# Transformer stack in float32, first block's mixer: another order of projection chunks and attention steps, turns one step later, grouped heads paired; extra constant matmuls at three places

## The reference, cut to what matters

```python
for l in range(DEPTH):                         # DEPTH = 2
    h = rms_norm(x, pre_mix_norm[l])
    proj = jnp.einsum('bsd,de->bse', h, w_in[l])       # 1024 -> 2464 columns
    (na_q, na_k, na_v, df_q, df_k, df_v, gq_q, gq_k, gq_v,
     ml_cq, ml_ckv, ml_kr) = jnp.split(proj, offsets, axis=-1)
    a_out = neighbourhood_attention(..., rel_bias[l])  # 4 heads of 64, with a bias
    b_out = diff_attention(dq[0], dq[1], dk[0], dk[1], ..., lam, slopes)
    b_out = rms_norm(b_out, diff_subln[l]) * (1.0 - lambda_init)
    c_out = gqa_attention(cq, ck, ...)                 # 4 query heads on 2 key heads
    d_out = mla_attention(q_nope, q_rope, k_nope, k_rope, mla_v)
    mix = jnp.concatenate([a_out, b_out, c_out, d_out], axis=-1)
    x = x + rms_norm(mix @ w_o[l], post_mix_norm[l])
    ...                                        # gated MLP, norm, residual
```

## Time and profile before

| | us |
|---|---|
| median of 3 runs | 1963.43 (1956.75 to 1965.12) |
| the profiled execution, its own time | 1959.28 |
| its span, first to last instruction | 1957.5 |
| PE busy in the span | 1867.2 (95%) |
| DVE busy | 1138.0 (58%) |
| ACT busy | 921.6 (47%) |
| mean granted TensorE clock | 0.981 |
| mixer of layer 0, from 84.67 to 132.91 | 48.24 |
| mixer of layer 1, from 430.22 to 481.12 | 50.90 |

### The profile page before, as it was taken

One profiled execution on the slowest core, in us unless ns is written; L12 is line 12 of the kernel. 1 busy time (PEld: TensorE's weight loads), 2 busy tenths in 40 slices (PEclk: granted clock), 3 DMA queues, 4 the chain that ended last, 5 costly groups with the idle time before them and its releaser, 6 DMA issues. The chain is left out here.

```text
span 1957.5 us, 29109 instructions
## 1 busy us (share of the span) xinstructions
PE 1867.2 (95%) x11568; PEld 1634.4 (83%) x11568; DVE 1138.0 (58%) x1647; ACT 921.6 (47%) x1267; POOL 175.0 (9%) x213
## 2 busy tenths in 40 slices
PE   7899999988999999899999999999889999989998
PEld 6668999766899978689998789998669998769997
DVE  6676555757655578554446465446765546765443
ACT  4564334456434446554435355345245435564342
POOL 1300000040000030001000001002501002000000
PEclk9999999999999999799999999999989999989999
DMA  7504555550355555126555425554725554524551
GB/s 249 181 22 147 175 183 185 181 172 12 129 193 193 191 187 180 49 87 215 176 204 177 172 86 175 201 182 169 219 90 172 173 202 147 203 91 173 181 204 66
DMA packets 185356, 313.08 MB, mean 160 GB/s; under 512 B 18877, under 2 KB 67571, under 8 KB 185267
## 3 DMA queue, kind: packets, MB, share of 16 engines
q1 hardware_dynamic: 182595, 304.24, 46.0%
q0 software_dynamic: 1376, 4.38, 0.9%
q10 hardware_dynamic: 1296, 3.24, 0.5%
HBM read 309.90 MB, written 1.94 MB: 159 GB/s over the span
## 5 line engine op out<-in xcount | busy, mean ns | idle before, releaser
L1459 DVE TENSOR_TENSOR w_lo<-raw,w_hi 128x2048 fp32r<-128x2048 f32 (+2 forms) x290 | 654.0, 2285 | 289.7 <-ACT w_hi L995 289.0
L995 ACT ACTIVATE w_hi<-raw 128x2048 fp32r<-128x2048 f32 (+2 forms) x290 | 533.5, 1877 | 107.5 <-PE tr L2010 59.8
L2008 PE MATMUL acc<-w_hi,hT_hi 128*128 128x512 f32 (+2 forms) x688 | 270.1, 393 | 13.3 <-DVE w_lo L1459 7.3
L2010 PE MATMUL acc<-w_hi,hT_lo 128*128 128x512 f32 (+2 forms) x688 | 266.4, 387 | 0.0
L2009 PE MATMUL acc<-w_lo,hT_hi 128*128 128x512 f32 (+2 forms) x688 | 266.3, 387 | 0.0
L2008 PE MATMUL acc<-w_hi,aux_hi 128*128 128x512 f32 x608 | 237.2, 390 | 0.0
L2009 PE MATMUL acc<-w_lo,aux_hi 128*128 128x512 f32 x608 | 237.2, 390 | 0.0
L2010 PE MATMUL acc<-w_hi,aux_lo 128*128 128x512 f32 x608 | 236.6, 389 | 0.0
L2008 PE MATMUL up<-hT_hi,w_hi 128*128 128x256 f32 x768 | 217.8, 284 | 0.6 <-DVE w_lo L1459 0.6
L2009 PE MATMUL tr<-hT_lo,w_hi 128*128 128x256 f32 x768 | 217.5, 283 | 0.0
L2008 PE MATMUL tr<-hT_hi,w_hi 128*128 128x256 f32 x768 | 217.5, 283 | 0.0
(11 more groups left out here) (361 smaller groups left out, 2761.1 us busy)
## 6 DMA issues: line engine op xcount, KB each, us to landing
raw<-in_mlp_w_up SPq DMA_DIRECT2D x64, 1024.0 KB, 6.6
raw<-in_mlp_w_down SPq DMA_DIRECT2D x64, 1024.0 KB, 5.4
raw<-in_ffn_w_gate_up SPq DMA_DIRECT2D x88, 512.0 KB, 4.8
raw<-in_ffn_w_down SPq DMA_DIRECT2D x22, 1024.0 KB, 5.1
raw<-in_w_in SPq DMA_DIRECT2D x16, 1024.0 KB, 8.2
raw<-in_sb_w_in SPq DMA_DIRECT2D x12, 1024.0 KB, 5.3
raw<-in_moba_w_in SPq DMA_DIRECT2D x12, 1024.0 KB, 5.3
raw<-in_nsa_w_in SPq DMA_DIRECT2D x10, 1024.0 KB, 6.3
```

The source lines that it names most:

```text
L995: nc.scalar.activation(w_hi[:, p0.slot, 0:p0.floats], raw[:, p0.slot, 0:p0.floats], ACT.Copy)\
L1459: nc.vector.tensor_tensor(w_lo[:, p0.slot, 0:m], raw[:, p0.slot, 0:m], f32(w_hi[:, p0.slot, 0:m]), ALU.subtract).then_inc(sem["lo_ready"], 1)
L2008: nc.tensor.matmul(dst, hi, whi, start=first, stop=False)
L2010: return nc.tensor.matmul(dst, lo, whi, start=False, stop=last)
```

## The change

1. The chunks of `w_in` are projected in the order (4, 3, 2, 1, 0). `jobs_early` now turns the differential q and k in place of the neighbourhood ones, which are the two late jobs now.
2. The scores of the first two steps are issued by PE inside the last chunk, behind `jobs_early` (`STEPS_EARLY = 2`); DVE (`steps_early`) and ACT take their maxima and exponentials there, ahead of emptying the last chunk.
3. The step order is DF and GQ, then NA, then ML. The turns are three steps behind the scores and the products four (`TURN_LAG = 3`). The two late jobs stand behind turn(1), ahead of out(0).
4. The differential norm is cut in three: ACT copies and squares (`od_taken`, now two increments), DVE reduces, takes the root and multiplies in three consecutive iterations; `diff_turn` stands in iteration 19 and writes the bank that the DF sums held.
5. The grouped heads are laid out so that the two heads of a step write different halves; POOL uses three additions in place of one for that.
6. ACT's exponential for `lam` moves from the mixer's head to behind chunk 3.
7. `keep_clock` is added in the last attention stage (10, ahead of the fifth turning job), in the stick-breaking stage (5, ahead of the first sums) and behind the convolution's variance (16).

```diff
-STEP_ORDER = (0, 1, 2, 3, 4, 5, 12, 6, 7, 13, 8, 9, 14, 10, 11, 15, 16, 17, 18, 19)
+STEP_ORDER = (4, 12, 5, 13, 6, 7, 14, 8, 9, 15, 10, 11, 0, 1, 2, 3, 16, 17, 18, 19)
+TURN_LAG = 3
...
+STEPS_EARLY = 2
...
-            g1 = add_gemm(plan, A["w_in"][l], D, A_IN, "proj", (4, 3, 0, 1, 2), {2: up_projections})
+            g1 = add_gemm(plan, A["w_in"][l], D, A_IN, "proj", (4, 3, 2, 1, 0), {2: up_projections})
...
-            g2.order = (0, 1, 4, 5, 2, 3, 6, 7)
+            g2.order = (4, 5, 2, 3, 0, 1, 6, 7)
...
+        def turn_index(j):
+            return JOBS_EARLY + j if j < STEPS_EARLY else JOBS_A + j
...
-                pair([head(half_rows(8 + t, HD * u, HD), half_rows(10, HD * u, HD), col("gq_v") + HD * u, HD * t, 4 + u)
-                      for u in range(2)])
+                pair([head(half_rows(8 + t, HD * u, HD), half_rows(10, HD * u, HD), col("gq_v") + HD * u,
+                           HD * (t if u == 0 else 1 - t), 4 + u) for u in range(2)])
```

ACT in the last chunk and in the mixer:

```diff
+                        for j in range(STEPS_EARLY):
+                            pair_exp(pair_steps()[j], j)
...
+                for i in range(STEPS_EARLY, len(steps) + TURN_LAG + 1):
                     if i < len(steps):
+                        pair_exp(steps[i], i)
+                    if 0 <= i - TURN_LAG < len(steps):
+                        j = i - TURN_LAG
...
+                    if i == STEPS_EARLY + TURN_LAG - 1:
+                        for j in range(JOBS_EARLY, JOBS_A):
+                            _, dst, scale = jobs_for("A")[j]
+                            evac_job(j + STEPS_EARLY, dst, scale, n["pt_ready"])
...
+                    if i == DF_LAST + 5:
+                        act.wait_ge(sem["o_done"], n["o_done"] + DF_LAST + 1)
+                        nc.scalar.activation(h[:, 0, 0:512], acc[:, 1, :], ACT.Copy).then_inc(sem["od_taken"], 1)
+                        nc.scalar.activation(h[:, 0, 512:1024], acc[:, 1, :], ACT.Square).then_inc(sem["od_taken"], 1)
+                    if i == DF_LAST + 8:
+                        act.wait_ge(sem["hT_tr"], n["hT_tr"] + 1)
+                        pair_out_hi((2, 3))
```

DVE (`steps_early` runs in the last chunk, before DVE empties its sums):

```diff
+            def steps_early(l):
...
+                for i in range(STEPS_EARLY):
+                    pair_max(steps[i], i)
+                    if i:
+                        pair_scaled(steps[i - 1], i - 1)
...
+                def diff_sums():
+
+                    dve.wait_ge(sem["od_taken"], n["od_taken"] + 2)
+                    sq = h[:, 0, 512:1024].rearrange("p (a c) -> p a c", c=HD)
+                    link(nc.vector.tensor_reduce(ss[:, 16:24], sq, AX_X, ALU.add))
...
+                    if i == DF_LAST + 5:
+                        diff_sums()
                     if i == DF_LAST + 6:
+                        diff_root()
+                    if i == DF_LAST + 7:
                         diff_gain()
...
+                    if i == DF_LAST + 8:
+                        pair_out_lo((2, 3), 4)
```

PE:

```diff
+                for i in range(STEPS_EARLY):
+                    pe.wait_ge(sem["pt_evac"], n["pt_evac"] + 2 * (i + 1))
+                    pair_scores(pair_steps()[i], i)
...
+                    if i == STEPS_EARLY + TURN_LAG - 1:
+                        late_jobs()
+                    if i == DF_LAST + 8:
+                        diff_turn()
+                    if i > TURN_LAG:
+                        j = i - TURN_LAG - 1
...
                         if j == ML_FIRST:
-                            pe.wait_ge(sem["od_taken"], n["od_taken"] + 1)
+                            pe.wait_ge(sem["hT_lo"], n["hT_lo"] + 4)
...
+                    if j == 4:
+                        pe.wait_ge(sem["evac_a"], n["evac_a"] - 1)
+                        pe.wait_ge(sem["evac_d"], n["evac_d"] - 1)
+                        keep_clock(acc[:, 0, 0:S], 10)
...
+                    if heads[0] == 0:
+                        keep_clock(acc[:, 0, 0:S], 5)
...
                 last.then_inc(sem["var_ready"], 1)
+                keep_clock(tr[:, 0, 0:S], 16)
```

More of the change, by code:

```diff
@@ L587, in pair_steps @@
                            A_IN + 128 * (2 * t + u) + 64, HD * u, 6 + t) for u in range(2)])
-            for i in range(GQ_STEPS.start, GQ_STEPS.stop):
-                steps[i]["apart"] = False
             return [steps[i] for i in STEP_ORDER]
@@ L1517, in gemm @@
                         turned_lo(ph.then, range(KT // 2))
+                    if ph.mix is not None and ph.mix.kind == "mixA" and i == 4:
+                        steps_early(ph.mix.l)
                     dve.wait_ge(sem["piece_used"], pieces[-1][0] + 1)
@@ new lines, in steps_early, with pair_max @@
+                for i in range(STEPS_EARLY):
+                    pair_max(steps[i], i)
+                    if i:
+                        pair_scaled(steps[i - 1], i - 1)
+            def pair_max(step, i):
+                slot = i % 4
+                dve.wait_ge(sem["s_ready"], n["s_ready"] + i + 1)
+                if step["bias"] is None:
+                    nc.vector.tensor_reduce(nmx[:, 2 * slot:2 * slot + 2], pair_banks(i), AX_X, ALU.min)\
+                        .then_inc(sem["s_max"], 1)
+                else:
+                    for u in range(2):
+                        ins = nc.vector.tensor_tensor_reduce(
+                            prob[:, slot, u, :], pair_bank(i, u), step["bias"][u], -step["scale"], -LOWEST, ALU.add,
+                            ALU.min, nmx[:, 2 * slot + u:2 * slot + u + 1])
+                    ins.then_inc(sem["s_max"], 1)
@@ new lines, in pair_scaled @@
+            def pair_scaled(step, i):
+                slot = i % 4
+                c = slice(2 * slot, 2 * slot + 2)
+                dve.wait_ge(sem["p_exp"], n["p_exp"] + 2 * (i + 1))
+                link(nc.vector.reciprocal(rec[:, c], den[:, c]))
+                p0, p1 = prob[:, slot, 0, :], prob[:, slot, 1, :]
+                r0, r1 = (rec[:, 2 * slot + u:2 * slot + u + 1] for u in range(2))
+                if step["diff"] is not None:
+                    mark(nc.vector.tensor_scalar(r1, r1, lam[:, 4:5], None, ALU.mult))
+                    link(nc.vector.tensor_scalar(p0, p0, r0, None, ALU.mult))
+                    nc.vector.scalar_tensor_tensor(out=p1, in0=p1, scalar=r1, in1=p0, op0=ALU.mult, op1=ALU.add)\
+                        .then_inc(sem["p_norm"], 2)
+                else:
+                    nc.vector.tensor_scalar(p0, p0, r0, None, ALU.mult).then_inc(sem["p_norm"], 1)
+                    nc.vector.tensor_scalar(p1, p1, r1, None, ALU.mult).then_inc(sem["p_norm"], 1)
@@ L2105, in jobs_early, with pair_scores @@
                     job(j, jobs_for("A")[j][0], n["pt_evac"])
+                for i in range(STEPS_EARLY):
+                    pe.wait_ge(sem["pt_evac"], n["pt_evac"] + 2 * (i + 1))
+                    pair_scores(pair_steps()[i], i)
+            def pair_scores(step, i):
+                for u, head in enumerate(step["heads"]):
+                    last = nc.tensor.matmul(pair_bank(i, u), head["q"][:, P * step["qt"]:P * step["qt"] + P], head["k"],
+                                            start=True, stop=True)
+                last.then_inc(sem["s_ready"], 1)
             def lag_turn():
@@ L2293, in mix_A @@
                 steps = pair_steps()
-                for i in range(len(steps) + 3):
+                for i in range(STEPS_EARLY, len(steps) + TURN_LAG + 1):
                     if i < len(steps):
                         step = steps[i]
-                        if i >= 2 and steps[i - 2]["bias"] is not None:
+                        if steps[i - 2]["bias"] is not None:
                             pe.wait_ge(sem["s_max"], n["s_max"] + i - 1)
-                        elif i >= 2:
+                        else:
                             pe.wait_ge(sem["p_exp"], n["p_exp"] + 2 * (i - 1))
-                        for u, head in enumerate(step["heads"]):
-                            last = nc.tensor.matmul(pair_bank(i, u), head["q"][:, P * step["qt"]:P * step["qt"] + P], head["k"],
-                                                    start=True, stop=True)
-                        last.then_inc(sem["s_ready"], 1)
-                    if i == 1:
-                        diff_jobs()
-                    if 2 <= i < len(steps) + 2:
-                        j = i - 2
-                        pe.wait_ge(sem["pt_evac"], n["pt_evac"] + JOBS_A + j - 1)
+                        pair_scores(step, i)
+                    if 0 <= i - TURN_LAG < len(steps):
+                        j = i - TURN_LAG
+                        pe.wait_ge(sem["pt_evac"], n["pt_evac"] + turn_index(j) - 1)
                         both_heads = steps[j]["diff"] is None
@@ L2332, in mix_A @@
                             for u in range(2):
-                                kv = (kt, u) if step["apart"] else (u, kt)
-                                head, at = step["heads"][kv[1]], P * (TT * kv[1] + kv[0])
```

(7 more changed lines are left out.)

145 lines of the change are left out of this document (50 added, 95 removed).

## The result

The changed kernel takes 1968.06 us (median of 20 runs, 1956.51 to 1971.34); the kernel before, on the same chip, 1961.51 (20 runs, 1956.70 to 1967.27). The ratio is 1.0030, 95% interval 1.0019 to 1.0041: slower by 0.3%, where 0.5% faster was forecast. The profiled execution of the changed kernel took 1969.47 us with a span of 1967.7, against 1959.28 and 1957.5 before.

The account below looks back on a forecast made before the run. PE, busy 95% of the span, was taken as the bound, with time to win in its waits and at 1.2 GHz. Terms 1.1 + 3.8 + 5.4 = 10.3 us gave 1953.0 us against 1963.43; range 1944 to 1960.

Parts of the forecast that it names:

- Early scores: First two steps' scores inside the last chunk: its end, E, comes 1.5 us later, hidden on DVE and ACT.
- The walk: Engine lists of a first-block mixer side by side: last chunk to first `w_o` matmul 45.6 us; kernel before 46.3.
- front: Mixer's start: two PE waits ahead of the late jobs, 1.2 and 1.7 us, replace the old 2.12 us wait.
- middle: Mixer's steps from scores(5) on: 1.84 us per step against 1.96 walked for the kernel before.
- end: Mixer's last part: three PE waits of 1.5, 1.6 and 1.8 us replace the old 3.11 us wait.
- Table load: ACT's table load leaves layer 1's mixer and is hidden behind chunk 3: 1.28 us won.
- Constants: `keep_clock` keeps full clock at no cost: 1.6 us won in stick-breaking, 2.3 last attention, 1.5 convolution, together 5.4.
- The sum of the first block: Both first-block mixers with PE at 2.4 GHz all along: 1.1 us won in layer 0, 3.8 in layer 1.
- the clock falls in the new waits: Rival, first-block mixers: a 3.4 us half-clock stretch costs 1.3 to 1.6, four take 5.5: 1958 us; chance 0.17.
- slower: Rival: clock falls at the mixers' front and stays down, over 0.5% slower, at most 1991 us; chance 0.06.
- The weighing of a rule: Skill's long-gap rule: first-block mixers' broken waits would keep 2.4 GHz, moving 0.17 to the forecast; prediction called this too strict.

Follow-up runs that it names:

- before_filled: Kernel before plus the three `keep_clock` constants, four calls in each first-block mixer's 2.12 us wait and six in its 3.11 us wait: 1944.87 us, ratio 0.9917.
- no_constants: Changed kernel without its three calls of `keep_clock` outside the first block: 1973.83 us, ratio 1.0058 to the kernel before.
- one_filled: Changed kernel with three `keep_clock` calls ahead of the first late job only: 1961.45 us, ratio 0.9997 to the kernel before.
- no_early: ends_filled without early scores, late jobs ahead of turn(0), nothing filled at the front: 1967.90 us, ratio 1.0033 to the kernel before.
- jobs_apart: Changed kernel with the two late jobs placed singly, behind product(2) and product(4): 1952.54 us, ratio 0.9948 to the kernel before.
- tall_scores: Changed kernel with differential scores over 64 rows a map instead of 32, giving other values: 1954.35 us, ratio 0.9958 to the kernel before.
- constants_only: Kernel before with only the three `keep_clock` calls (5, 10 and 16) of the change added: 1955.88 us, ratio 0.9972.
- ends_filled: Changed kernel with three `keep_clock` calls in each of the five new waits of a first-block mixer: 1946.07 us, ratio 0.9923 to the kernel before.

## Why the prediction was wrong

1. **Early scores**: E 1.66 us later for a forecast 1.5. Right. What they give back was never priced apart; measured at full clock it is 1.3.
2. **The walk** (front, middle, end): right. All waits came within 0.3 us of their forecast at full clock, and the mixer at 1.00 took 45.90 us for 45.6. The walk of the kernel before was right too: 46.3 forecast, 46.07 in before_filled. What was to be won in layer 0 was thus only the half clock at the old end.
3. **Table load**: gone, as forecast, and worth 1.44 (before_filled's two layers), nearer the 1.28 of the row than the 2.66 that the Trainium skill's figures (ScalarE: Activation LUTs, "What ACT_TABLE_LOAD costs") would make.
4. **Constants**: 5.4 forecast, 4.3 and 5.8 measured; place by place 1.6, 1.5 and 2.3 forecast, 1.5, 1.5 and 2.1 in the aligned traces. Right.
5. **The sum of the first block**: "with PE at 2.4 GHz all along". This step failed. 0.7 us were to be won there in layer 0 (48.24 - 1.66 - 45.90) and 3.3 in layer 1; the clock took 12.1 in each.
6. **The price of the rival "the clock falls in the new waits"** failed with it. The mechanism was right and had 0.17; but I took the length of a fall, 3.4 us, from the earlier trace rows. The one at the front of layer 1 there was over before that order's first 32-row scores came; the changed order puts such scores right behind its waits. With them a fall at the front lasted 30.7 or 37.5 us in all eight mixers of the changed kernel, no_constants, one_filled and no_early (the last with before's own wait), and 13.7 and 3.4 in jobs_apart; tall_scores shows the part of the rows alone. Even in the old order 3.4 was the short end, as constants_only's 10.2 and 13.7 show; one execution's row was no bound.
7. **The rival "slower"** had the place and sign and a chance of 0.06, though not the size: it meant 0.5% and the whole mixers at 1.2 GHz, and it was 0.3% and 37.5 of 58 us in each. "PE busy over 85% in the mixer speaks against it" was no argument: PE was busy for 36.07 of 37.5 us at 0.50, and all through one_filled's 30.70. Its price of 0.41 us per us of stretch was 0.32, since at full clock PE waits for ACT and DVE part of the time that half clock fills. With that, 75 us of stretch cost 24.2: 1949.0 + 24.2 = 1973.2 for the profiled execution. It took 1969.47; most of the rest is the two stretches, 1.9 us and some of 2.8, that before had by chance.
8. **The weighing of a rule.** I wrote that by the Trainium skill (TensorE: Matmul & The Clock Gate, "HAM oscillation"), which warns of long unbroken gaps, these broken waits would keep 2.4 GHz. The trace contradicts that reading: in the changed kernel the first wait of 1.42 us was enough, and in no_early one of 2.00. The same page's "A second HAM failure mode: psum-queue depth-cycling" tells of short, frequent idle times between groups of matmuls that do so; that is the nearer rule, and I did not weigh it.

Shown is: the clock makes the slowdown (filling the waits takes it away), and the 32-row scores prolong it. That the waits start it rests on where the falls are: in the traces of this study the clock falls 29 times in a first-block mixer, 28 of them inside a PE wait of 1.33 us or more or at most 1.8 us behind its end (the other 3.0 behind one of 1.33, in jobs_apart, with a wait of 0.49 between), and never where the waits are filled. A fill also adds full-height matmuls, and no run tells whether the idle time or the thin work around it would do it alone. Open is why the same kernel loses more in some executions than in others, why tall_scores still has 13.7 us, and the stretch of 27.3 us at 0.50 near 780 us, which every kernel of this study has and none touched.

## What to carry to other kernels

When a change moves waits and work about, price the clock by what stands behind each wait in the new order, not by how long falls lasted in the old one: a fall that heals in 3 to 14 us behind one kind of matmul may last a whole stage behind a thinner kind, with PE looking fully busy. Short waits on PE of 1 to 3 us are cheap to cover with dummy matmuls that end just ahead of what is waited for, and this is worth trying before any reordering: here it gave 17 us to the old order (4 of them in the three constants) and 22 to the new. Where a wait can be removed instead (the late jobs behind products whose bank is free), do both.

## What was unexpected of the hardware

- A fully busy PE does not bring the clock back by itself: 30.70 of 30.70 us busy at 0.50 (one_filled), with turns, products, and scores of 32 and 64 rows.
- The same instructions over 64 rows instead of 32 shortened it to 13.7 and 6.8 us, and sixteen full-height matmuls in a block ended it inside the block.
- A single wait of 1.3 to 2.0 us can be enough for the fall, and whether it is, and for how long, differs between executions of one kernel: the changed kernel's mean clock lay between 0.971 and 0.985, and ends_filled, with all waits filled, spread over 1.3 us in six runs where the changed kernel spread over 14.8 in twenty.
